# Router logits: which operand is stationary, and how the selection reads them

## The reference

```python
def moe_swiglu(h, router, w_gate, w_up, w_down):
    xf = h.reshape(N, D)                         # N = 512, D = 1024
    logits = (xf @ router).astype(jnp.float32)   # router: 1024 x 8
    top_v, top_i = lax.top_k(logits, TOP_K)      # TOP_K = 2
    gates = jax.nn.softmax(top_v, axis=-1)
    ...
```

## Time and profile before

| | |
|---|---|
| median of 3 executions | 1085.34 us (1085.24 to 1087.74) |
| the profiled execution | 1085.57 us |
| its span, first to last instruction | 1084.0 us |
| mean granted TensorE clock | 0.977 |
| busy: TensorE matmul / weight load | 1016.2 us (94%) / 873.0 us (81%) |
| busy: VectorE / ScalarE / GpSimd | 601.6 / 463.5 / 64.1 us |
| chain that ended last: TensorE / VectorE / DMA | 85% / 6% / 4% |

### The profile page before, as it was taken

The page is one execution under the profiler, slowest core; times in us unless marked ns, Lnnn a source line. Parts: engine busy times, 40 slices in busy tenths (PEclk is TensorE's granted clock), DMA queues, the critical chain, the costliest instruction groups (busy, mean ns, idle before and its releaser), DMA issues.

```text
span 1084.0 us, 15218 instructions
## 1 busy us (share of the span) xinstructions
PE 1016.2 (94%) x5492; PEld 873.0 (81%) x5492; DVE 601.6 (55%) x780; ACT 463.5 (43%) x606; POOL 64.1 (6%) x134
## 2 busy tenths in 40 slices
PE   5999999999999999999999779999999999999980
PEld 4887888888888888888888679999787888878870
DVE  5585676354434434344447600100789989888885
ACT  5535564244222222323225100100677777777772
POOL 2200000000010000000000020000000000000003
PEclk9999999999999999999999899999899999999995
DMA  8021312436273644536323099999999999999976
GB/s 278 2 78 40 135 60 89 125 98 191 79 216 110 207 129 139 154 114 177 94 73 83 1 327 295 254 285 282 386 350 389 372 389 369 366 392 369 391 284 243
DMA packets 172468, 228.03 MB, mean 210 GB/s; under 512 B 16852, under 2 KB 118228, under 8 KB 172432
## 3 DMA queue, kind: packets, MB, share of 16 engines
q1 hardware_dynamic: 160640, 189.03, 53.3%
q0 software_dynamic: 10400, 35.87, 9.6%
q10 hardware_dynamic: 1392, 2.64, 0.6%
HBM read 201.12 MB, written 26.39 MB: 210 GB/s over the span
## 4 chain that ended last, share of the span: by engine, by line
PE 85%; DVE 6%; DMA 4%; ACT 2%; issue 2%; SPq 0%; POOL 0%; DVEq 0%; ACTq 0%; POOLq 0%
PE bank L1108 22%; PE bank L1109 22%; PE bank L1110 22%; PE bank L1506 7%; PE bank L1520 3%; PE bank L1280 1%; DMA u_raw<-in_moe_w_down 1%; DMA stage_own<-in_moe_w_up 1%; PE bank L1484 1%; PE bank L1120 1%; PE bank L1410 1%; PE bank L1260 1%; PE bank L1271 1%; PE bank L1605 1%; DVE w_lo L1676 1%
## 5 line engine op out<-in xcount | busy, mean ns | idle before, releaser
L2109 DVE TENSOR_TENSOR u_lo<-u_raw,u_hi 128x2048 fp32r<-128x2048 f32 (+1 forms) x112 | 226.1, 2055 | 11.8 <-ACT u_hi L991 11.7
L991 ACT CAST u_hi<-u_raw 128x2048 fp32r<-128x2048 f32 (+1 forms) x113 | 194.5, 1731 | 61.1 <-DMA u_raw<-in_moe_w_up 30.2
L1108 PE MATMUL bank<-big_hi,w_lo 128*128 128x512 f32 (+2 forms) x352 | 134.5, 382 | 0.0
L1109 PE MATMUL bank<-big_lo,w_hi 128*128 128x512 f32 (+2 forms) x352 | 134.4, 382 | 0.0
L1110 PE MATMUL bank<-big_hi,w_hi 128*128 128x512 f32 (+2 forms) x352 | 134.3, 382 | 0.0
L1676 DVE TENSOR_TENSOR w_lo<-stage_own,w_hi 128x1024 fp32r<-128x1024 f32 (+1 forms) x91 | 105.5, 1203 | 13.5 <-ACT w_hi L745 13.4
L1108 PE MATMUL bank<-u_hi,nx_lo 128*128 128x512 f32 (+1 forms) x288 | 107.8, 374 | 0.0
L933 ACT ACTIVATE scratch<-bank 128x512 f32<-128x512 f32 x21 | 12.6, 599 | 218.8 <-PE bank L1110 218.8
L1109 PE MATMUL bank<-u_lo,nx_hi 128*128 128x512 f32 (+1 forms) x288 | 105.5, 366 | 0.0
L1110 PE MATMUL bank<-u_hi,nx_hi 128*128 128x512 f32 (+1 forms) x288 | 105.3, 366 | 0.0
L1933 DVE TENSOR_TENSOR scratch<-scratch,bank 128x512 f32<-128x512 f32 x21 | 14.5, 688 | 151.6 <-ACT scratch L933 151.6
(11 more groups left out here) (284 smaller groups left out, 1713.9 us busy)
## 6 DMA issues: line engine op xcount, KB each, us to landing
u_raw<-in_moe_w_down SPq DMA_DIRECT2D x60, 512.0 KB, 6.8
u_raw<-in_moe_w_gate SPq DMA_DIRECT2D x53, 512.0 KB, 7.7
u_raw<-in_moe_w_up SPq DMA_DIRECT2D x53, 512.0 KB, 8.6
stage_own<-in_ffn_w_gate SPq DMA_DIRECT2D x21, 512.0 KB, 6.0
stage_own<-in_ffn_w_up SPq DMA_DIRECT2D x21, 512.0 KB, 7.2
stage_own<-in_ffn_w_down SPq DMA_DIRECT2D x21, 512.0 KB, 3.9
xbuf<-scratch POOLq DMA_DIRECT2D x21, 496.0 KB, 6.2
stage_own<-in_moe_w_gate SPq DMA_DIRECT2D x20, 512.0 KB, 5.7
```

The source lines that it names most:

```text
L991: s.copy(u_hi[u % HIS][0:rows, 0:size], u_raw[u % RAWS][0:rows, 0:size]).then_inc(n_hi, 1)
L1108: t_.matmul(dst, st_lo, mv_hi, start=start, stop=False, skip_group_check=check)
L1109: t_.matmul(dst, st_hi, mv_lo, start=False, stop=False, skip_group_check=check)
L2109: v.tensor_tensor(u_lo[u % RAWS][0:rows, 0:size], u_raw[u % RAWS][0:rows, 0:size], u_hi[u % HIS][0:rows, 0:size], ALU.subtract).then_inc(n ...
```

## The change

`logits` exchanges the operands. The turned tile's block, 128 x 128, is stationary, and the router's block, 128 x 8, moves. The result is tokens by logits, written to `bank[2][:, 8 t : 8 t + 8]`, where the four transposes left it before. The VectorE copy, the four transposes, the view `logitsT` and two semaphores go; the selection waits for the last logits matmul itself.

```diff
--- before.py
+++ after.py
@@ -258,7 +258,6 @@
         f_act = view(5120, 1024, 2)
         xnT = [view(4096 + 1024 * n, 1024, 8) for n in range(2)]
         pscale = view(6144, 1024)
-        logitsT = qr_now[0:E, :]
         iota_c = cos_t[:, :, :].rearrange("p t n -> p (t n)")[:, 0:C]
         chosen_x = view(4096, T * C, T)
         route = view(7168, 1024)
@@ -386,8 +385,6 @@
         mix_done = sem("mix_done")
         h_mix = sem("h_mix")
         pool_scaled = sem("pool_scaled")
-        logitsT_done = sem("logitsT_done")
-        logitsT_ready = sem("logitsT_ready")
         logits_done = sem("logits_done")
         sel_ready = sem("sel_ready")
         chosen = sem("chosen")
@@ -1436,9 +1433,9 @@
                 pe.wait_ge(xnT_hi, 2 * T + t + 1)
                 pe.wait_ge(xnT_lo, 2 * T + t + 1)
                 for k in range(KD):
-                    last = t_.matmul(bank[2][0:E, tok(t)], router[:, k, :], xnT[t % 2][:, k, :], start=k == 0, stop=k == KD - 1)
+                    last = t_.matmul(bank[2][:, t * E:(t + 1) * E], xnT[t % 2][:, k, :], router[:, k, :], start=k == 0, stop=k == KD - 1)
                 if t == T - 1:
-                    last.then_inc(logitsT_done, 1)
+                    last.then_inc(logits_done, 1)
 
             pe.wait_ge(router_landed, 16)
             pe.wait_ge(z_lo, 4)
@@ -1456,11 +1453,6 @@
                 rows_T(t)
                 logits(t - 1)
             logits(T - 1)
-            pe.wait_ge(logitsT_ready, 1)
-            for t in range(T):
-                last = t_.transpose(bank[2][:, t * E:(t + 1) * E], logitsT[:, tok(t)], ident[0:E, 0:E])
-            last.then_inc(logits_done, 1)
-
 
             pe.wait_ge(chosen, 1)
             for t in range(T):
@@ -1994,8 +1986,6 @@
             norm_rows(3 * T + 3, 3)
             rows_T(2)
             rows_T(3)
-            dve.wait_ge(logitsT_done, 1)
-            v.tensor_copy(logitsT, bank[2][0:E, :]).then_inc(logitsT_ready, 1)
 
 
             def tab(n, width=T * E):
```

## The result

| | before | changed |
|---|---|---|
| median | 1085.29 us (6 runs) | 1091.12 us (1089.72 to 1091.69, 6 runs) |
| ratio, 95% interval | | 1.0044 (1.0034 to 1.0055) |
| the profiled execution, its span | 1085.57, 1084.0 us | 1091.69, 1090.1 us |
| mean granted clock | 0.977 | 0.971 |

What follows compares the result with a forecast made beforehand. TensorE was taken as the bound, with nothing covering the router's chain of waits. Terms -1.18 - 0.07 + 0.5 = -0.7 us, plus 5.2 for the clock, gave +4.5 on 1085.34: 1089.8 us, 8-in-10 range 1084.0 to 1091.5.

Steps and rivals of the forecast that it cites:

- 0.52 against 0.37: Router logits: chance that the clock falls, against the rival that it stays up, which would give 1084.6 us.
- Removed, 1.18 us: Between last logits matmul and selection: without copy, transposes and their hand-overs, 1.18 us less.
- The further 0.07 for a shorter last matmul: Last logits matmul: moving 8 columns instead of 128 takes 202 ns against 273 ns, 0.07 us less.
- The pace of the pairs, 0.12 us: Logits at full clock: a load and matmul pair every 0.12 us, where 0.109 us was the pace before.
- the term of +0.5 us: Logits at full clock: 48 exchanged pairs on the chain cost 0.5 us more, bounds -0.4 and +3.9.
- Loads in series: Logits rival, chance 0.06: every load waits for the matmul before it, at 0.19 us, giving 1088.0 us.
- the gather's escape from its slow clock: Gather rival, chance 0.05: the clock rises before or soon after the gather starts, saving up to 2.4 us: 1082.2 us.
- The clock falls, halfway through the second tile's 16 pairs, about 603.1: Second tile's logits: almost nothing moves, so the clock drops to 1.2 GHz there; chance of a fall 0.52.
- The early end of the range: Before the second tile's transposes: a fall before 601.1 slows 8 more pairs and 8 more transposes, +6.2 us, 1091.5 us.
- The price of the fall, 5.2 us: Logits after the fall: 40 pairs at 0.23 us and 8 slower transposes cost 5.2 us more.
- Nothing is lost or won behind: From the gather on: it begins 4.5 us later, partly at low clock as before, so nothing is counted there.
- TensorE runs without gaps behind the transfers: After the first expert's weight transfers, the largest ending at 649.75 us: TensorE has no gaps; no term in the sum.

Runs made afterwards that it cites:

- Experiment 1: The changed kernel with the router's eight columns read sixteen times over, so 128 columns move: 1086.25 us, 0.9999 of the kernel before; repeated, 1085.64 us, 0.9988.
- changed_again: The changed kernel run again, unaltered, beside the kernel before in a later set of runs: 1090.62 us, ratio 1.0030.
- the delays: The kernel before with 14 or 28 repeated small VectorE instructions ahead of the selection: 1089.60 us, ratio 1.0033, and 1092.86 us, ratio 1.0055.
- move128: The changed kernel with 128 moving columns, the router's eight read sixteen times over; two comparisons with the kernel before: 1086.25 us, 0.9999, and 1085.64 us, 0.9988.
- second set: The second of three sets of follow-up runs, on one chip with the kernel before beside it, which took 1082.73 to 1089.80 us in 25 executions.
- move128_fill_again: Second comparison of the changed kernel with 128 moving columns plus 12 and 5 unread matmuls around the rank counts, against the kernel before: ratio 0.9985.

## Why the prediction was right

Slower by over 0.3%, 1089.8 us, was forecast, with 1087.2 to 1091.5 as that case's own range; 1091.12 us was measured. The mechanism was right: the logits at the low clock outweigh what the removed copy and transposes save, and the delay reaches the end. That the clock would fall was a choice, at 0.52 against 0.37, since no row could settle it, and the time came within 0.4 us of the range's upper end; two of the six executions (1091.65 and 1091.69) lie above it. Step by step:

- **Removed, 1.18 us**: right. 0.04 us is left of 1.22. The further 0.07 for a shorter last matmul was wrong: the matmuls of 8 columns are recorded with 256 ns (361 at the low clock), only the first of a tile with 175. That the others are longer because they wait for their loads is a reading, not a measurement.
- **The pace of the pairs, 0.12 us**: too high. (1.85 - 0.256) / 15 = 0.106 us at 1.00, so the term of +0.5 us was 48 x (0.106 - 0.109) = -0.1, and the loads overlap better than L1461's: a pair comes 84 ns sooner than its load of 190 would allow by itself, not 67. The Trainium skill, "TensorE: Matmul & The Clock Gate", section "LDWEIGHTS (loading the stationary operand)", says that a load takes its columns over 1.2 in ns, which makes 107 for 128 columns; the pace at 1.00 agrees with it. So the rule speaks for the change, where the prediction has it against. At 0.50 the pace does not agree with it: there pairs come every (6.83 - 0.36) / 31 = 0.209 us, where the forecast had 0.23. Loads in series, the second rival, are refuted. So is the gather's escape from its slow clock, the third: the clock is at 0.50 until 623.9, inside the gather.
- **The clock falls, halfway through the second tile's 16 pairs, about 603.1**: 603.42 in one execution, 602.25 in the other. Experiment 1 shows that it is this fall that costs, and that it doesn't come where 128 columns move beside the same loads. The moment was in part luck: it moves by 1.2 us between two executions of the same program. The early end of the range, a fall by the wait at 600, did not come: the transposes from 601.33 ran at 1.00, 8 in 1.06 us.
- **The price of the fall, 5.2 us**: too high for the first execution, met in the second. In the first the second tile's logits cost 0.33 more (602.23 to 604.41 for 602.13 to 603.98), the transposes 0.72 (606.15 - 604.41 for 605.00 - 603.98), the last 32 pairs 6.83 - 3.66 = 3.17: together 4.2. Less the 1.18, and less 0.09 because the second tile's logits follow their transposes sooner, that is the +2.95 of the table; the forecast was +4.5. In changed_again, where the clock fell earlier than was forecast, the three are 1.28, 0.72 and 3.17, together 5.2, and the selection starts 3.90 later.
- **Nothing is lost or won behind**: held by the delays and the second run of the changed kernel, within their intervals; the first comparison's +3.7 to +6.0 us is more than that execution's start explains. That execution loses 3 us more behind the selection, in a stretch where the forecast put nothing: there the wait for the first expert's weights was longer, as TensorE's timeline shows, and the clock fell once more, as two windows show.

```profile
654.14 3.78 PE L1498 MATMUL bank<-scratch,stage_own 128*128 128x144 f32 x16 [3.09 <-DMA stage_own<-in_moe_w_up]
```

The windows:

```profile
654.00:655.00 1.00, 0.85 (x5) 0.86 (x6) 0.00 (x0) 0.00 (x0) 0.00 (x0) 0.81 1.10 280
655.00:658.00 3.00, 3.00 (x15) 3.00 (x14) 0.00 (x0) 0.04 (x1) 0.00 (x0) 0.50 0.94 306
```

Before, the matmuls of that place start at 649.80 after 1.78 us of waiting and take 2.23. So of the 3 us, 654.14 - 649.80 - 3.14 = 1.20 lie in the transfers and 3.78 - 2.23 = 1.55 in the fall, which move128 has too without being slower. What sets either in a given execution was not settled, nor how much of them the later table brings on. That the forecast is so near to the median is in part luck: for the profiled execution the pace and the price of the fall were put 1.5 us too high together, and a loss of 3 us behind the selection was left out. The prediction's statement that TensorE runs without gaps behind the transfers is also too strong: its own show waits of 1.89 and 2.35 us near 764 and 787; nothing in the sum hung on it.

## What to carry to other kernels

Where a matmul's small side can be either operand, look at what each choice moves, not only at how long the engine is busy: with 8 columns moving beside full loads the engine was as busy as before and its clock fell all the same, and the logits behind the fall took 6.83 us instead of 3.66. Reading the small operand sixteen times over, as the moving side, kept the clock and cost little here: 3.74 us for the last 32 matmul records, where 3.66 were needed before the change. But it did not make the kernel clearly faster than it had been. A short chain that makes the table for later transfers passes a delay to the end about one for one; whether 2.4 us saved in a gather beside it are kept has to be measured by itself, and was not settled here.

## What the runs showed that was not expected

- The kernel before is not equally steady everywhere: 1084.98 to 1087.74 us in the 6 executions of the table on the result, 1082.73 to 1089.80 in the 25 of the second set. 1.1 us can't be told there with 12 executions of the other kernel.
- In the profiled execution of the kernel before, SyncE issued the first dependent weights 6.6 us after the table (630.23 for 623.58); in the others it was 4.0 us, but for move128_fill_again with 5.2. The wait for `in_moe_w_up` in the transfer stretch nevertheless ended 26.2 us after the table in the former (649.80), and 27.3 to 29.2 us after it in both executions of the changed kernel, both of move128 and the two delays. SyncE's first issue in the changed kernel, from its timeline:

```profile
630.72 0.37 SPq L448 DMA_DIRECT2D stage_own<-in_moe_w_down  x1
```

- The transposes between such logits neither kept the clock up nor brought it back: 8 of them ran at 1.00 from 601.33, ahead of the fall, and 8 at 0.50 from 604.41 to 606.15. The Trainium skill, "TensorE: Matmul & The Clock Gate", section "Part 4: PE-mode transpose", says that transposes don't count as busy in the same way; no run here separates them from the logits around them.
